# A projection's first half in another order, and T sums made from PSUM, in a two-block kernel on one core

## What is computed

```
attn = dilated_mixture_attention(q, k, v_a)
sgu = spatial_gating(u, v_s, ...)
mixed = concatenate([rms_norm_2(attn, attn_out_norm[l]), rms_norm_2(sgu, sgu_out_norm[l])], -1)
y = mixed @ w_out[l]
x = x + rms_norm_2(y, post_mix_norm[l])
h = rms_norm_2(x, pre_ffn_norm[l])
f = (silu(h @ w_gate[l]) * (h @ w_up[l])) @ w_down[l]
x = x + rms_norm_2(f, post_ffn_norm[l])
```

## Time and profile before

| | |
|---|---|
| Median of 3 runs | 2080.42 us (2078.24 to 2081.92) |
| Profiled execution | 2081.29 us |
| Its span | 2079.5 us |
| PE busy | 2004.0 us, 96% |
| DVE, ACT, POOL busy | 1325.6, 846.2, 960.3 us |
| Mean granted TensorE clock | 0.987 |
| HBM traffic | 193 MB, 93 GB/s over the span |

### The profile page before, as it was taken

One profiled execution on the slowest core, in us unless ns is written; L12 is line 12 of the kernel. 1 busy time (PEld: TensorE's weight loads), 2 busy tenths in 40 slices (PEclk: granted clock), 3 DMA queues, 4 the chain that ended last, 5 costly groups with the idle time before them and its releaser, 6 DMA issues.

```text
span 2079.5 us, 27399 instructions
## 1 busy us (share of the span) xinstructions
PE 2004.0 (96%) x10021; PEld 1662.3 (80%) x10021; DVE 1325.6 (64%) x1744; ACT 846.2 (41%) x1349; POOL 960.3 (46%) x564
## 2 busy tenths in 40 slices
PE   7999999999999999999999899897999999999997
PEld 6888888888887778878887689775788888878885
DVE  7887777756637655874331543799665656657977
ACT  5444544434420034560202676566333332334443
POOL 1344555332233477733542200848755555435552
PEclk8999999999999999999999999999999999999998
DMA  9223212211122143242111000231333323346344
GB/s 282 69 81 112 100 53 95 85 30 41 41 62 62 61 172 112 102 142 63 50 40 59 23 1 1 71 116 58 120 107 106 111 90 102 120 171 229 101 140 150
DMA packets 178925, 193.98 MB, mean 93 GB/s; under 512 B 9799, under 2 KB 122904, under 8 KB 178842
## 3 DMA queue, kind: packets, MB, share of 16 engines
q1 hardware_dynamic: 172420, 178.53, 26.9%
q10 hardware_dynamic: 6422, 14.37, 1.9%
HBM read 151.71 MB, written 41.16 MB: 93 GB/s over the span
## 4 chain that ended last, share of the span: by engine, by line
PE 79%; DVE 11%; ACT 5%; issue 3%; POOL 2%; ACTq 0%; DMA 0%; SPq 0%; DVEq 0%; POOLq 0%
PE psum L994 6%; PE psum L996 6%; PE psum L995 6%; PE psum L1533 6%; PE psum L1534 6%; PE psum L1535 6%; PE psum L1155 3%; PE psum L1632 3%; PE psum L1634 3%; PE psum L1633 3%; PE psum L1015 3%; PE psum L1016 3%; PE psum L1014 3%; PE psum L1436 3%; PE psum L1310 2%
## 5 line engine op out<-in xcount | busy, mean ns | idle before, releaser
L777 POOL TENSOR_TENSOR w_hi<-w_raw,ones 128x1024 fp32r<-128x1024 f32 x60 | 149.3, 2489 | 480.9 <-PE psum L996 356.7
L994 PE MATMUL psum<-h_hi,w_hi 128*128 128x512 f32 x704 | 284.1, 404 | 0.0
L996 PE MATMUL psum<-h_hi,w_lo 128*128 128x512 f32 x704 | 274.7, 390 | 0.0
L995 PE MATMUL psum<-h_lo,w_hi 128*128 128x512 f32 x704 | 274.2, 390 | 0.0
L1664 ACT ACTIVATE arena<-psum 128x1024 f32<-128x1024 f32 (+7 forms) x134 | 100.3, 752 | 215.6 <-PE psum L996 134.0
L780 POOL TENSOR_TENSOR w_lo<-w_raw,w_hi 128x1024 fp32r<-128x1024 f32 x60 | 167.9, 2799 | 4.7
L995 PEld LDWEIGHTS psum<-h_lo,w_hi 128*128 128x128 f32 x704 | 132.4, 188 | 28.4 <-issue 2.6
L994 PEld LDWEIGHTS psum<-h_hi,w_hi 128*128 128x128 f32 x704 | 132.3, 188 | 28.4 <-issue 2.6
L996 PEld LDWEIGHTS psum<-h_hi,w_lo 128*128 128x128 f32 x704 | 132.1, 188 | 28.5
L1632 PE MATMUL psum<-w_hi,h_hi 128*128 128x512 f32 x308 | 122.0, 396 | 8.1 <-DVE h_lo L3220 5.1
L1633 PE MATMUL psum<-w_lo,h_hi 128*128 128x512 f32 x308 | 121.5, 394 | 0.0
(11 more groups left out here) (483 smaller groups left out, 5315.6 us busy)
## 6 DMA issues: line engine op xcount, KB each, us to landing
w_raw<-w_in SPq DMA_DIRECT2D x64, 512.0 KB, 3.8
act_op<-arena SPq DMA_DIRECT2D x77, 256.0 KB, 2.2
arena<-act_op SPq DMA_DIRECT2D x77, 256.0 KB, 2.7
w_raw<-w_gate SPq DMA_DIRECT2D x22, 512.0 KB, 4.0
w_raw<-w_up SPq DMA_DIRECT2D x22, 512.0 KB, 5.1
arena<-ada_w SPq DMA_DIRECT2D x16, 512.0 KB, 7.2
arena<-w_out SPq DMA_DIRECT2D x16, 512.0 KB, 6.0
out_T<-arena SPq DMA_DIRECT2D x16, 512.0 KB, 5.6
```

Source lines behind the costliest of these rows:

```text
L994: pe.matmul(o, wh, xh, start=(k == 0), stop=False)
L995: pe.matmul(o, wh, xl, start=False, stop=False)
L996: return pe.matmul(o, wl, xh, start=False, stop=(k == KT - 1))
```

## The change

It has four parts, and the total of matmuls is the same.

1. In the projection's first half, DVE makes only one of P1's four low parts before the attention's last head and one after the scalings; the copies 1 and 3 (DVE) and 0 and 2 (ACT) go between steps 4 to 7; the S2 sums follow step 7 all together; POOL makes T4 four steps later and S1 first; ACT rounds P7's B side before the statistics and loads the sqrt table before copy 4. PE transposes slices 2 and 3 after two token tiles of step 3 instead of three.
2. T1, T3 and T2 are made by DVE directly from the PSUM banks that hold B12 and B22, right behind their low parts; T3 and S3 change their sign; the raw copy of B22 is dropped. PE may overwrite the banks when T2 is made.
3. The low parts of T3 and half of T2's move from POOL to DVE, T4 is summed at the end; the last row scaling goes to ACT; `whole(0..3)` moves ahead of the weight sums.
4. Pair 1 has the product order A11, A12, S4, S1, S3, S2, A22; the transposes of B12/B22 for three token tiles start before the fourth is normed, and the transposes for k = 2 and 3 stand behind the plain step 0 and 1 instead of ahead of them.

```
-SECOND_PRODUCTS = ["A11", "A12", "S4", "S2", "S1", "S3", "A22"]
+SECOND_PRODUCTS = ["A11", "A12", "S4", "S1", "S3", "S2", "A22"]
-Q_POOL = {"T3": 0, "T2": QJ, "T1": 2 * QJ, "S3": 3 * QJ, "T4": 4 * QJ, "S1": 5 * QJ, "S4": 6 * QJ}
+Q_POOL = {"T3": 0, "T2": QJ, "T1": 2 * QJ, "S3": 3 * QJ, "S1": 4 * QJ, "T4": 5 * QJ, "S4": 6 * QJ}
...
 (POOL)
                 if n == 7:
                     for i in range(QJ):
+                        q_sum("S1", i)
+                if n == 11:
+                    for i in range(QJ):
                         q_sum("T4", i)
-                    for i in range(QJ):
-                        q_sum("S1", i)
...
 (PE, projection)
-                        if (n, t) == (3, 3):
+                        if (n, t) == (3, 2):
...
 (PE, b_transpose)
-                    pe.wait_ge(x_ready["B12"], k - 1)
-                    pe.wait_ge(x_ready["B22"], k - 1)
-                    pe.wait_ge(b22_taken, 4 * (k - 1))
+                    pe.wait_ge(b22_taken, 3 * (k - 1))
+                    pe.wait_ge(t_sum, 3 * (k - 1))
...
             for k in range(4):
                 pe.wait_ge(x_ready["B12"], k + 1)
                 pe.wait_ge(x_ready["B22"], k + 1)
-                if k < 2:
-                    b_transpose(k + 2)
                 plain_k("g2", "A11", "B12", k, k == 0, False)
...
                 mm = plain_k("u2", "A22", "B22", k, False, k == 3)
+                if k < 2:
+                    b_transpose(k + 2)
...
 (ACT, projection)
+                if n in (5, 7):
+                    q_raw_copy(n - 5)
...
 (ACT, instead of the loop over k with both raw copies)
+            def b_taken(k):
+                act.wait_ge(tr_full, T_BASE[4] + KT + 2 * k + 2)
+                for e, name in enumerate(("B12", "B22")):
+                    src = psum[:, 4 + (2 * k + e) % 4, :]
+                    A(x_hi[name][:, k, :], src, ACT.Identity, scale=mul(k + 4 * e)).then_inc(b22_taken, 1)
+                    if name == "B12":
+                        A(r12[:, k, :], src, ACT.Identity, scale=mul(k)).then_inc(b22_taken, 1)
...
 (DVE, projection)
-            q_raw_copy(1)
-            q_raw_copy(3)
+            q_lo(3, "P1", 3)
             dve.wait_ge(row_in, 48)
             for n in Q_ORDER_A[4:]:
                 q_lo(n, O_PRODUCTS[n // QJ], n % QJ)
-                if 4 <= n < 8:
-                    q_s2(n - 4)
+                if n in (4, 6):
+                    q_raw_copy(n // 2 * 2 - 3)
+                if n == 7:
+                    for j in range(QJ):
+                        q_s2(j)
...
 (DVE, T sums)
                 dve.wait_ge(s0_done, S0_BASE + k + 1)
-                TT(r11[:, k, :], r12[:, k, :], r11[:, k, :], ALU.subtract).then_inc(t_sum, 1)
-                dve.wait_ge(t_sum, 2 * k + 1)
-                TT(t2_raw[:, k, :], r22[:, k, :], r11[:, k, :], ALU.subtract).then_inc(t_sum, 1)
+                STT(r11[:, k, :], b12, mul(k), r11[:, k, :], ALU.mult, ALU.subtract).then_inc(t_sum, 1)
+                STT(r22[:, k, :], b22_, mul(k + 4), r12[:, k, :], ALU.mult, ALU.subtract).then_inc(t_sum, 1)
+                dve.wait_ge(t_sum, 3 * k + 1)
+                STT(t2_raw[:, k, :], b22_, mul(k + 4), r11[:, k, :], ALU.mult, ALU.subtract).then_inc(t_sum, 1)
...
             for k in range(4):
-                TT(r22[:, k, :], r12[:, k, :], r22[:, k, :], ALU.subtract).then_inc(t_sum, 1)
...
+                dve.wait_ge(t_rounded, 3 * k + 2)
+                TT(x_lo["T3"][:, k, :], r22[:, k, :], x_hi["T3"][:, k, :].bitcast(F32), ALU.subtract).then_inc(x_ready["T3"], 1)
```

More of the change, by code:

```diff
@@ L928, in product_raw, with whole, second_lo, t_lo @@
                 return a_raw(name, par) if name[0] == "A" else s_raw[name]
+            def whole(k):
+                x, r = ("B11", "B21")[k // 4], (r11, r21)[k // 4]
+                pool.wait_ge(lo_done, T_BASE[4] + k + 1)
+                TT(r[:, k % 4, :], x_hi[x][:, k % 4, :].bitcast(F32), x_lo[x][:, k % 4, :].bitcast(F32), ALU.add).then_inc(s0_done, 1)
+            def second_lo(name):
+                hi, lo = w_slot(name)
+                pool.wait_ge(gw_hi, SECOND_PRODUCTS.index(name) + 1)
+                TT(lo, product_raw(name, 1), hi.bitcast(F32), ALU.subtract).then_inc(gw_ready, 1)
+            def t_lo(name, raw, ks, turn):
+                for k in ks:
+                    pool.wait_ge(t_rounded, turn(k))
+                    TT(x_lo[name][:, k, :], raw[:, k, :], x_hi[name][:, k, :].bitcast(F32), ALU.subtract).then_inc(x_ready[name], 1)
+            for k in range(4):
+                whole(k)
             for s in range(2, 4):
@@ L2111, in _ @@
                 if n == N - 1:
+                    A(lb_tmp, ones[:, 0:8], ACT.Sqrt)
                     q_raw_copy(4)
@@ L2117, in _ @@
                 q_hi_a(j, "P1", j)
-            A(lb_tmp, ones[:, 0:8], ACT.Sqrt)
+            for j in range(QJ):
+                q_hi_b(QJ + j, "P7", j)
             act.wait_ge(ao_done, 2 * NT)
@@ L2209, in _, with t_hi @@
             q_root(5)
-            for name in ("A11", "A12", "S4"):
-                second_hi(name)
+            second_hi("A11")
+            q_xn(5, 3, 2)
             act.wait_ge(spilled_a, 16 * 4)
             act.wait_ge(spilled_b, 16 * 2)
-            for k in range(4):
+            def b_taken(k):
                 act.wait_ge(tr_full, T_BASE[4] + KT + 2 * k + 2)
-                for e, (name, raw) in enumerate((("B12", r12), ("B22", r22))):
+                for e, name in enumerate(("B12", "B22")):
                     src = psum[:, 4 + (2 * k + e) % 4, :]
                     A(x_hi[name][:, k, :], src, ACT.Identity, scale=mul(k + 4 * e)).then_inc(b22_taken, 1)
-                    A(raw[:, k, :], src, ACT.Identity, scale=mul(k + 4 * e)).then_inc(b22_taken, 1)
+                    if name == "B12":
+                        A(r12[:, k, :], src, ACT.Identity, scale=mul(k)).then_inc(b22_taken, 1)
+            def t_hi(k):
+                for a, (name, raw) in enumerate((("T1", r11), ("T3", r22), ("T2", t2_raw))):
+                    act.wait_ge(t_sum, 3 * k + a + 1)
+                    copy(x_hi[name][:, k, :], raw[:, k, :]).then_inc(t_rounded, 1)
+            b_taken(0)
+            b_taken(1)
+            second_hi("A12")
             act.wait_ge(gp_done, 1)
             A(silu_of[0], psum[:, P_BANK["g1"], :], ACT.Silu).then_inc(silu_a_done, 1)
-            for a, name, raw in ((2, "T2", t2_raw), (1, "T1", r11)):
-                for k in range(4):
-                    act.wait_ge(t_sum, 2 * k + a)
-                    copy(x_hi[name][:, k, :], raw[:, k, :]).then_inc(t_rounded, 1)
+            second_hi("S4")
+            b_taken(2)
+            t_hi(0)
+            b_taken(3)
+            for k in range(1, 4):
+                t_hi(k)
             act.wait_ge(spilled[1], 16 * 2)
@@ L2229, in _ @@
             act.wait_ge(gp_done, NPR)
-            second_hi("S2")
-            second_hi("S1")
-            for k in range(4):
-                act.wait_ge(t_sum, 8 + k + 1)
-                copy(x_hi["T3"][:, k, :], r22[:, k, :]).then_inc(t_rounded, 1)
-            second_hi("S3")
-            second_hi("A22")
+            for name in ("S1", "S3", "S2", "A22"):
+                second_hi(name)
             for k in range(4):
@@ L3009, in _ @@
             q_raw_copy(7)
-            for j in range(QJ):
+            q_lo(0, "P1", 0)
+            attended(2 * NT - 1)
+            for j in range(1, 3):
                 q_lo(j, "P1", j)
-            attended(2 * NT - 1)
             def q_s2(j):
```

89 lines of the change are left out of this document (39 added, 50 removed).

## The result

The changed kernel takes 2070.1 us (median of 6 runs, 2068.96 to 2071.69) against 2081.06 (6 runs, 2078.24 to 2084.95): ratio 0.9946, 95% interval 0.9936 to 0.9956. It is 11.0 us faster, where 18.0 were forecast, and lies 1.1 us above the range.

What follows compares the result with a forecast made beforehand. PE is busy 2004.0 of 2079.5 us, so only pauses and slow clock can be won back. 7.8 (Part A) + 10.2 (Part B) = 18.0 off 2081.29 gives 2063.3; the median, 0.87 lower, is 2062.4; range 2059 to 2069.

Steps and rivals of the forecast that it cites:

- Part A: Projection's first half: 7.8 us gained (bounds 7.2 and 8.2), step 12 starting at 1342.1 instead of 1350.23.
- The scalings ... are then ready at 1311.1: Scalings that PE's transposes wait for: ready at 1311.1 instead of just before 1312.81; transposes start 1.05 us sooner.
- ACT rounds P7's B parts in the gap before: Rounding on ACT ahead of the attention statistics, in a gap.
- one low part of 1.62 us fewer: DVE ahead of the attention statistics: three low parts in all, one of 1.62 us fewer than before.
- What is late next: ... a pause of 0 to 1.0. I take 0.4: Projection step 12: DVE's low part 14 and bank-freeing sum run beside POOL, 1.7 instead of 0.7 us; pause taken as 0.4.
- The pause before step 4: Projection: step 4 waits for raw copy 2 behind step 11's B rounding, starting at 1320.2; a pause of 2.0 us left.
- The 3.9 us pause at step 5: Projection: DVE's low parts 4 to 7 come before any S2 sum, so this pause and its slow clock go.
- the table load ahead of copy 4: ACT: a 1.28 us load makes copy 4 end 1.0 us later, at 1296.2; costed at nothing.
- Part B: B12/B22 and T sums, through pair 1 to pair 2: 10.2 us gained (bounds 6 and 12.7).
- The sums from PSUM: DVE's T sums with one PSUM input: about 0.7 us each, 3.35 us per k for five operations, POOL at 1.27.
- Rival 1: Clock falls at a pause left (step 4 or before plain step 0): costs 2.4 to 2.9 us, 2065; chance 0.12.
- the granted clock is 1.00 from step 4 to the end of pair 1: Sign of the forecast: no 1.2 GHz stretch on PE from projection step 4 through pair 1.

Runs made afterwards that it cites:

- x1: The changed kernel with POOL starting the low parts of P7's B side only behind the scalings: 2066.95 us, ratio 0.9930.
- x2: The kernel before, with only ACT's rounding of P7's B side moved ahead of the attention statistics: 2080.56 us, ratio 0.9999.
- x11: The changed kernel with POOL waiting for the scalings and raw copy 2 ahead of step 11's B rounding, no idle transposes: 2067.22 us, ratio 0.9931.
- x8: x7 with raw copy 2 moved ahead of the B rounding of step 11: 2066.14 us, ratio 0.9927.
- x6: Part B of the change alone, with the projection as in the kernel before: 2071.11 us, ratio 0.9958.
- x12: The changed kernel itself, timed once more: 2070.81 us, ratio 0.9950.
- x4: The changed kernel with 20 idle transposes on PE ahead of the first plain product: 2066.68 us, ratio 0.9932.
- x7: The changed kernel with both POOL's wait of x1 and the idle transposes of x4: 2067.28 us, ratio 0.9933.
- x9: x8 with all four U3 sums on DVE in one go behind the low part of step 17: 2066.14 us, ratio 0.9927.
- x5: Part A of the change alone, with gate and up as in the kernel before: 2079.40 us, ratio 0.9994.
- x3: The changed kernel with ACT's rounding of P7's B side moved back behind the scalings: 2069.67 us, ratio 0.9943.

## Why the prediction was wrong

**Part A failed, at the step "The scalings ... are then ready at 1311.1".** They began at 1310.50 and were ready only at 1315.7; this trace was 0.97 us late before the stage, so that is 1314.8 on the forecast's clock, 3.7 late. The greater part is in the scalings themselves, 5.26 us for 1.68. "ACT rounds P7's B parts in the gap before" was costed at nothing; on ACT that is right, and what it lets POOL start was not asked. The smaller part is in front of them: they began 0.57 us sooner than before instead of the 1.62 of "one low part of 1.62 us fewer", because the 128x8 row ahead of them, come earlier, fell beside POOL's S3 sums (1.25 us for 0.17). That part x1 does not mend. x1 and x2 show the cause from both sides: POOL's low parts taken away, 1.67 us for the four scalings; the early rounding put into the kernel before, 5.20. The traces also show that it is not only operations with two SBUF inputs: the scalings have one input from SBUF and a column of numbers. The Trainium skill (SBUF — State Buffer, SBUF: two separate sides, and Who interferes with whom) says that GpSimd and VectorE shut each other out also where VectorE is in a 2-port performance mode, which a tensor_scalar can enter. The trace agrees, with 0.42 us for one scaling with POOL idle and 1.32 beside it; the mode itself no trace names. The prediction drew on that section for the sums and did not put the scalings to it.

**Part A's size was out of reach beyond that.** "What is late next: ... a pause of 0 to 1.0. I take 0.4" looked at step 12 alone. There it was right (0.36 us, L3040). But DVE's low parts up to step 18 run beside POOL too. With the scalings mended and copy 2 first, step 12 starts where the forecast had it (44.82 against 44.7 us, or 45.1 with its pause of 0.4), and 2.5 us of the 8.0 are given back at step 16 (x11). In x8 it is 3.3, by the low clock behind that pause. The best that part A reached is 5.6 us (98.24 to 92.68), under its lower bound of 7.2.

**The pause before step 4** was mis-sized a little: 1.72 us idle for the 2.0 forecast, and its cause, copy 2 behind the B rounding, is confirmed by x8 (1.25 with the copy first). The 3.9 us pause at step 5 with its slow clock is gone, as said, and the table load ahead of copy 4 cost nothing: the load is 1.28 us with the next operation directly behind it, and the copy ends at 1297.1, or 1296.2 on the forecast's clock, as its sum had it and not 1297.6.

**Part B was right.** Without a slow stretch it gave 10.6 us (x6) and 11.0 (x12) for 10.2; pair 1 starts 2.8 us sooner for 2.5 (x6), has no pauses at S1, S3 and S2, and the pauses left are 0.72 at T4 and 0.72 at the start of pair 2 for 1.3 + 0.5 + 0.7. The sums from PSUM took what the nearest row had said (five per k), and POOL beside them the short time:

```profile
L3172 DVE SCALAR_TENSOR_TENSOR h_lo<-psum,cols,h_hi 128x512 fp32r<-128x512 f32 x4 | 3.0, 742 | 0.0
L3174 DVE SCALAR_TENSOR_TENSOR arena<-psum,cols,arena 128x512 f32<-128x512 f32 x4 | 3.0, 741 | 0.0
...
L939 POOL TENSOR_TENSOR w_lo<-w_raw,w_hi 128x512 fp32r<-128x512 f32 x2 | 2.6, 1286 | 0.1
```

**Rival 1 came true in part.** The clock fell behind the pause before the plain product in four traces of seven, for 1.6 us where 2.4 to 2.9 had been priced, and 0.12 had been given to it because "pauses of 2.3 and 2.9 left it alone". One trace in which a pause does no harm says little: in the same kernel, at the same pause, it fell once and once not. The sign "the granted clock is 1.00 from step 4 to the end of pair 1" failed by this (0.52 behind 1419.08). Behind the pause at the output's transposes, which the forecast did not have, it fell as well.

Of the 7.0 us that are missing in the median, the profiled execution shows 5.0 in part A and 1.2 in part B, where 10.6 less 1.6 of slow clock are 9.0; 0.97 more it had lost before the stage began. Together these are 7.2.

## What to carry to other kernels

- When work is moved earlier on one engine, ask which engine it sets free to start, and what runs beside that. Here a rounding that cost ACT nothing made four short VectorE scalings three times as long through GpSimd.
- When a long pause goes, look further than the next wait: with the scalings mended PE came 8 us sooner to step 12, and VectorE, for which it had paused only 0.6 us from there on before, took 2.5 to 3.3 us back. Moving four sums in its queue only moved the pause, and made it longer.
- The version to keep is the changed kernel with GpSimd's wait (2066.95 us, against 2070.1 and 2070.8 for the changed kernel), with copy 2 first or without: it has the shorter projection in every trace without the moved sums (92.7 to 93.5 us for 95.5 to 96.2). The medians of x1, x4, x7, x8, x9 and x11, 2066.1 to 2067.3, cannot be told from each other.

## What the runs showed of the hardware

- A VectorE scaling of 128x512 from SBUF to SBUF takes 0.42 us with GpSimd idle and 1.32 beside its subtractions; a 128x8 operation of the same kind 0.17, and 1.25 beside its sums. So in these traces the price goes by the neighbour's operations, not by its own size.
- Pauses of TensorE of 2.3 to 3.0 us lower the clock in some executions and not in others of the same code: behind 2.96 to 2.98 us at the output's transposes it fell in the changed kernel and in x5, and not in x4 and x12; behind 2.31 and 2.32 us at step 16 it fell in x1, x3, x7 and x8, and behind 2.33 not in x11.
- With this kernel, five executions of one program spread over 0.9 us (x3) to 4.7 us (x9), so a difference of 1 us between two medians, as between x8 and x11, settles nothing.
